# A mixture-of-experts decoder trunk on one core: the first expert's rows by one-hot products on the normed rows in SBUF

## Chip, cores, metric

The kernel runs on one core of one Trainium2 chip. The metric is the time of one execution on the device in microseconds (us); lower is better.

## What is computed

The input is 512 tokens (four tiles of 128, T = 4) of 1024 float32 features. There are two layers: gated linear attention, then forgetting attention, each followed by a grouped mixture of 16 experts of which each token takes two. The channel mixer is what the change touches:

```python
def grouped_moe(x, router_w, router_bias, w_gate, w_up, w_down):
    scores = softmax(x @ router_w); sel = scores + router_bias
    ...  # best group of 4 experts by the sum of its top 2, then the top 2 in it
    gates = sum(one_hot(expert_idx, N_EXPERTS) * w[..., None], axis=1)
    h = silu(einsum('td,edf->tef', x, w_gate)) * einsum('td,edf->tef', x, w_up)
    return einsum('tef,efd->td', h * gates[..., None], w_down)
```

Before it stands `h = layer_norm(ALPHA * h + mix, ...)`, after it `h = layer_norm(ALPHA * h + ffn, ...)`. The kernel computes each expert only for the tokens that picked it.

## The kernel before

One program per engine, written out by hand; semaphores join them, and each engine runs its instructions in order. SyncE loads weights, GpSimd gathers and scatters rows, TensorE multiplies, ScalarE and VectorE split every float32 operand into a high part (a cast to fp32r, by ScalarE) and a low part (the rest, by VectorE). A product of two such operands is three fp32r products (`products`, lines 717 to 719).

**Weights.** An expert has three matrices (gate, up, down), each in two halves of 1 MB. SyncE's `experts` (line 506) issues the 96 halves of a layer in the order gate 0, up 0, gate 1, up 1, down 0, gate 2 and so on, into eight raw halves of a ring. Halves 0 to 7 wait for the ring to be free, half 4 also for the stores of the normed rows (`last_rows_stored`), half 6 also for the first gather (line 499). From half 8 on, each waits for the half eight before it to be used (`half_used`). ScalarE casts a half (`high_half`, line 1346), VectorE takes its low part (`low_half`, line 1613), then TensorE may use it.

**Entry to the experts**, once in each layer. The last tile's norm ends; its rows stand in SBUF as `Hp` (tokens on partitions), and GpSimd stores all rows in DRAM as `h_rows` (line 593). TensorE computes the router's logits (line 822) and fills its time with products that nobody reads (`idle_products`, line 797). VectorE's `router` selects two experts per token with some twenty small instructions; ScalarE's Exp (line 1329) stands among them. `picked_b` goes to TensorE, which sums ranks (line 833: how many tokens up to this one picked the expert) and totals (line 836). VectorE masks the ranks (line 1774) and compares them with 1 to 128 (`one_hots4`, line 2233): for an expert a table of token by slot, 128x512. Four small products of this table with `info` (row numbers and gates) give the tokens of the slots (line 878, columns 0 and 1, `ids_done`) and, later, their gates (columns 2 and 3). VectorE turns them into row numbers `tokv` (line 1721) and `tokg` (line 1833).

**Rows of an expert.** GpSimd gathers 128 rows from `h_rows` by `tokv` into `xg` (line 607), which lies over the first two tiles of `Hp` and is cleared by two memsets first (line 586), since slots without a token are not written. TensorE transposes them in eight steps (`turn_rows`, line 885) into PSUM banks 0 and 1, ScalarE casts them (line 1356), VectorE takes the low part (line 1827), and `xgT` is ready: the gate product may start. At the entry, the gathers of experts 0 and 1 go out at once, that of expert 2 when expert 0 is transposed.

**The expert loop.** TensorE's order for expert e is: gate e, transposes of the rows of e+1, up e, down e-1, transposes of the hidden rows of e (`turn_hidden`, line 894, which waits for VectorE's gated product, line 1856), table of e+3 (line 870). ScalarE also writes the scaled residual to `sum_rows` in DRAM (line 1365), on which the experts' results are scattered with addition.

Of the kernel before, what the change touches and what calls it, by code (L numbers as in the profile page):

```python
# [5 lines left out]
F32 = mybir.dt.float32  # L6
# [4 lines left out]
ALU = mybir.AluOpType  # L11
ACT = mybir.ActivationFunctionType
AX = mybir.AxisListType
# [30 lines left out]
def yoco_trunk(nc, x, gla_w_in, gla_w_gk, gla_b_gk, gla_norm_g, gla_w_out, kv_w, forget_bias, fox_w_qg,  # L44
# [88 lines left out]
    with ctx:  # L133
# [116 lines left out]
        ranks = at(17792, T, E)  # L250
# [5 lines left out]
        IDS_BANKS = (7, 2, 3)  # L256
# [6 lines left out]
        rt = [at(14656 + 64 * n, T, E) for n in range(12)]  # L263
        rs = [at(14656 + 64 * 12 + 16 * n, T, GROUPS) for n in range(8)]
        rv = [at(14656 + 64 * 14 + 4 * n, T) for n in range(8)]
        total = at(14656 + 64 * 14 + 32, E)[0:1, :]
# [36 lines left out]
        pads_clear = sem("pads_clear")  # L303
        moves = sem("moves")
        hot, ids_done, tbl_done, tbl_ev = sem("hot"), sem("ids_done"), sem("tbl_done"), sem("tbl_ev")
# [146 lines left out]
        def _(sp):  # L452
# [35 lines left out]
            def experts(L):  # L488
                for n in range(HALVES):
# [4 lines left out]
                    elif n < RAW_HALVES:  # L494
# [3 lines left out]
                        if n == 6:  # L498
                            sp.wait_ge(gathered[0], 16 * (8 * L + 1))
# [27 lines left out]
        def _(pool):  # L527
# [54 lines left out]
            def clear_pads(L):  # L582
                pool.wait_ge(first_rows_stored, 32 * (L + 1))
                pool.wait_ge(h_scaled, T * L + 2)
                for n in range(2):
                    pool.memset(xg[:, n, :], 0.0).then_inc(pads_clear, 1)

            def layer_norm_rows(N):

                for t in range(T):  # L590
# [4 lines left out]
                    if t == 2:  # L595
                        clear_pads(N // 2)
# [105 lines left out]
        def _(pe):  # L702
# [91 lines left out]

            def idle_products(n, bank):
# [31 lines left out]
            def router(L):  # L827
                idle_products(20, 4)
                pe.wait_ge(rt_picked, L + 1)
                for t in range(T):  # L830
                    for s in range(t + 1):
                        before = upto_b if s == t else ones_b
                        pe.matmul(ps[:, 6, t * E:(t + 1) * E], before[:, :], picked_b[:, s, :],
                                  start=s == 0, stop=s == t)
# [4 lines left out]
                idle_products(5, 4)  # L839
# [22 lines left out]
            def experts(L):  # L862
# [13 lines left out]
                def entry_table(e, what, dst):  # L876
                    for s in range(T):
                        mm = pe.matmul(dst, onehot_of(e)[:, s * P:(s + 1) * P], info[:, s, e, what],
# [1382 lines left out]
```

## Time and profile before

| | us |
|---|---|
| median of the timed runs | 1234.52 |
| timed runs, lowest and highest | 1226.4, 1235.66 |
| the profiled execution's own time | 1230.52 |
| its span (first to last instruction) | 1228.8 |
| TensorE busy in it | 1193.8 (97%) |
| VectorE busy | 893.2 (73%) |
| ScalarE busy | 703.7 (57%) |
| GpSimd busy | 183.9 (15%) |

The span is what the trace shows; the time also holds what lies around it. Starts in the trace count from the span's start. Layer 0 enters its experts at about 250 to 285, layer 1 at about 890 to 925. PE is TensorE's matmuls, PEld its weight loads, DVE is VectorE, ACT ScalarE, POOL GpSimd, SPq SyncE's queue; "q" behind an engine is its sequencer. "x8" behind an entry is the number of records merged in it; a bracket at the end tells how long the engine was idle before it and what ended that.

### The profile page before, as it was taken

The numbers are of one execution on the slowest core, as the hardware profiler recorded it, in microseconds if no ns is written. First come the engines' busy times: TensorE is split into PE (matmuls) and PEld (weight loads), VectorE is DVE, ScalarE is ACT, GpSimd is POOL, SyncE is SP. The second block draws the span as 40 slices with busy tenths as digits, with TensorE's granted clock in tenths as the row PEclk, the third lists the DMA queues.
The fourth block names the chain that finished last, engine by engine and source line by source line (L and its number), as shares of the span: only waits on it lengthen the run. The fifth ranks groups of instructions, "written<-read, shape, count | busy, mean of one in ns | idle before, by whom it ended". The sixth has DMA issues, their size and how long they took to land.

```text
span 1228.8 us, 14990 instructions
## 1 busy us (share of the span) xinstructions
PE 1193.8 (97%) x5802; PEld 945.0 (77%) x5803; DVE 893.2 (73%) x1159; ACT 703.7 (57%) x866; POOL 183.9 (15%) x158
## 2 busy tenths in 40 slices
PE   7999999999999999999999999999999999999995
PEld 5787588877888888876887766768878888888873
DVE  5275555678999998989433555675679999998886
ACT  4432523357687786774333554573267778777672
POOL 1000100211132221210000000000212222122111
PEclk9999999999999999999899999999999999999998
DMA  8223021179999999987111420322289999999973
GB/s 286 71 85 122 1 103 70 52 257 411 358 368 378 368 370 377 358 340 281 69 70 52 154 86 18 103 84 88 78 314 381 373 362 376 379 367 371 370 276 137
DMA packets 66346, 281.52 MB, mean 229 GB/s; under 512 B 12854, under 2 KB 13110, under 8 KB 41698
## 3 DMA queue, kind: packets, MB, share of 16 engines
q1 hardware_dynamic: 49248, 247.55, 53.2%
q0 software_dynamic: 12288, 28.42, 8.1%
q10 hardware_dynamic: 4738, 4.57, 1.1%
q8 instruction: 47, 0.77, 0.3%
q14 instruction: 25, 0.20, 0.0%
HBM read 270.99 MB, written 25.20 MB: 241 GB/s over the span
## 4 chain that ended last, share of the span: by engine, by line
PE 83%; DMA 7%; DVE 6%; issue 2%; ACT 1%; POOL 0%; DVEq 0%; SPq 0%; ACTq 0%; POOLq 0%
PE ps L717 22%; PE ps L719 22%; PE ps L718 22%; DMA ring<-in_moe_w_up_dram 4%; PE ps L885 2%; PE ps L1168 2%; PE ps L1178 2%; DVE ring_r L1613 2%; PE ps L1191 2%; DMA ring<-in_moe_w_down_dram 1%; PE ps L894 1%; DMA ring<-in_kv_w_dram 1%; PE ps L822 1%; PE ps L1099 1%; PE ps L1087 1%
## 5 line engine op out<-in xcount | busy, mean ns | idle before, releaser
L1613 DVE TENSOR_TENSOR ring_r<-ring,ring_r 128x2048 fp32r<-128x2048 f32 x128 | 291.7, 2284 | 7.8 <-ACT ring_r L1346 7.8
L1346 ACT CAST ring_r<-ring 128x2048 fp32r<-128x2048 f32 x128 | 242.6, 1927 | 15.7 <-DMA ring<-in_moe_w_gate_dram 9.8
L718 PE MATMUL ps<-ring_r,xgT_r 128*128 128x512 f32 x528 | 205.9, 390 | 0.0
L1346 ACT CAST high_r<-ring 128x2048 fp32r<-128x2048 f32 x64 | 122.2, 1913 | 113.4 <-DMA ring<-in_moe_w_up_dram 113.4
L1613 DVE TENSOR_TENSOR ring_r<-ring,high_r 128x2048 fp32r<-128x2048 f32 x64 | 146.1, 2289 | 36.3 <-ACT high_r L1346 35.9
L613 POOL DMA_INDIRECT sum_rows<-arena,tokv x28 | 57.7, 2062 | 389.6 <-ACT arena L1399 389.6
L718 PEld LDWEIGHTS ps<-ring_r,xgT_r 128*128 128x128 f32 x528 | 99.3, 188 | 18.8
L717 PE MATMUL ps<-ring_r,xgT_r 128*128 128x512 f32 x272 | 109.1, 401 | 0.2 <-DVE ring_r L1613 0.2
L719 PE MATMUL ps<-ring_r,xgT_r 128*128 128x512 f32 x272 | 106.1, 390 | 0.0
L717 PE MATMUL ps<-high_r,xgT_r 128*128 128x512 f32 x256 | 102.9, 402 | 1.2 <-DVE xgT_r L1827 1.1
L717 PE MATMUL ps<-featT,ring_r 128*128 128x512 f32 x256 | 103.8, 405 | 0.0
L717 PE MATMUL ps<-ring_r,featT 128*128 128x512 f32 x256 | 102.4, 400 | 0.0
L1607 DVE TENSOR_TENSOR ring_r<-ring,ring_r 128x1024 fp32r<-128x1024 f32 x72 | 84.4, 1221 | 23.3 <-ACT ring_r L1259 23.3
L718 PE MATMUL ps<-ring_r,featT 128*128 128x512 f32 x256 | 100.3, 392 | 0.0
L719 PE MATMUL ps<-ring_r 128*128 128x512 f32 x256 | 100.3, 392 | 0.0
L719 PE MATMUL ps<-high_r,xgT_r 128*128 128x512 f32 x256 | 100.1, 391 | 0.0
L719 PE MATMUL ps<-featT,ring_r 128*128 128x512 f32 x256 | 100.1, 391 | 0.0
L718 PE MATMUL ps<-ring_r 128*128 128x512 f32 x256 | 99.8, 390 | 0.0
L717 PE MATMUL ps<-ring_r,hidT_r 128*128 128x512 f32 x240 | 93.8, 391 | 1.0 <-DVE ring_r L1613 1.0
L719 PE MATMUL ps<-ring_r,hidT_r 128*128 128x512 f32 x240 | 93.5, 390 | 0.0
L718 PE MATMUL ps<-ring_r,hidT_r 128*128 128x512 f32 x240 | 93.4, 389 | 0.0
L607 POOL DMA_INDIRECT arena<-h_rows,tokv x32 | 70.6, 2205 | 69.9 <-DVE tokg L1821 37.9
(288 smaller groups left out, 2118.8 us busy)
## 6 DMA issues: line engine op xcount, KB each, us to landing
ring<-in_moe_w_gate_dram SPq DMA_DIRECT2D x64, 1024.0 KB, 12.2
ring<-in_moe_w_up_dram SPq DMA_DIRECT2D x64, 1024.0 KB, 13.0
ring<-in_moe_w_down_dram SPq DMA_DIRECT2D x64, 1024.0 KB, 12.4
ring<-in_gla_w_in_dram SPq DMA_DIRECT2D x6, 2048.0 KB, 9.8
ring<-in_kv_w_dram SPq DMA_DIRECT2D x4, 2048.0 KB, 12.8
ring<-in_fox_w_qg_dram SPq DMA_DIRECT2D x4, 2048.0 KB, 8.1
ring<-in_gla_w_out_dram SPq DMA_DIRECT2D x2, 2048.0 KB, 7.8
h_rows<-arena POOLq DMA_DIRECT2D x8, 512.0 KB, 2.9
```

Source lines behind the costliest of these rows:

```text
L607: pool.indirect_dma_start(out=dst, out_offset=None, in_=h_rows, in_offset=bass.IndirectOffsetOnAxis(ap=rows, axis=0), bounds_check=last_ro ...
L613: pool.indirect_dma_start(out=sum_rows, out_offset=bass.IndirectOffsetOnAxis(ap=rows, axis=0), in_=src, in_offset=None, bounds_check=last_ ...
L717: pe.matmul(o, left[0], right[0], start=k == 0, stop=False)
L718: pe.matmul(o, left[0], right[1], start=False, stop=False)
L719: return pe.matmul(o, left[1], right[0], start=False, stop=k == n_k - 1)
L885: mm = pe.transpose(ps[:, kk, j * P:(j + 1) * P], src[:, (4 * kk + j) * P:(4 * kk + j + 1) * P], ident[:, :])
L1168: pe.matmul(ps[:, SCORE + a, 0:(i + 1) * P], kq[rows, p % 3, 1, i * P:(i + 1) * P], kq[rows, p % 3, 0, 0:(i + 1) * P], start=True, stop=Tr ...
L1178: mm = pe.transpose(ps[:, TURNED + a, n * P:(n + 1) * P], prob[:, s % 3, a, n * P:(n + 1) * P], ident[:, :])
L1191: mm = pe.matmul(ps[a * DH:(a + 1) * DH, VALUE, n * P:S], v_b[:, n, c:c + DH], prob_t[:, a, n, n * P:S], start=n == 0, stop=n == T - 1, sk ...
L1346: act.copy(high, w).then_inc(half_high, 1)
L1607: dve.tensor_tensor(low, w, high.bitcast(F32), ALU.subtract).then_inc(w_low, 1)
L1613: dve.tensor_tensor(low, w, high.bitcast(F32), ALU.subtract).then_inc(half_low, 1)
```

## The change

The rows of each layer's first expert (expert 0) are no longer gathered and transposed. TensorE multiplies `Hp`, still in SBUF, with expert 0's one-hot table: for each of the eight feature blocks, the sum over four token tiles of a product with 128x128 stationary and 128 moving float32 columns. The result is expert 0's rows already transposed, in banks 0 and 1. Around it:

- The table of expert 1 is the first one, behind the products; those of expert 2 and 0 stand behind expert 0's gate. Row numbers and gates are taken from one product of four columns. The first gather is that of expert 1, the next that of expert 2. Each has its wait: the one for expert 1 for all direct products (`xt_done`), since `xg` lies over `Hp`.
- The memsets of `xg` go. SyncE's half 6 waits for the gather of expert 1 (`gathered[1]`).
- ScalarE casts half 2 ahead of Exp and half 3 behind the row numbers of `info`; both casts stood behind the router.
- VectorE takes the low parts of halves 2 and 3 behind expert 0's rows, with the small table instructions around them.
- Five fillers after the ranks become four, and the fillers between and behind the tables go. The router's scratch moves from the arena to the place of `turned`.

```diff
             def router(L):
                 idle_products(20, 4)
                 pe.wait_ge(rt_picked, L + 1)
...
                 mm.then_inc(rt_ranks, 1)
-                idle_products(5, 4)
+                idle_products(4, 4)
...
+            def direct_rows(kk, tiles):
+
+                for j in range(4):
+                    c = slice(j * P, (j + 1) * P)
+                    for t in tiles:
+                        mm = pe.matmul(ps[:, kk, c], Hp[:, t, (4 * kk + j) * P:(4 * kk + j + 1) * P],
+                                       onehot_of(0)[:, t * P:(t + 1) * P].bitcast(F32),
+                                       start=t == 0, stop=t == T - 1, skip_group_check=True)
+                return mm
...
+                pe.wait_ge(hot, E * L + 1)
+                for kk in range(2):
+                    direct_rows(kk, range(EARLY, T)).then_inc(xt_done, 1)
                 pe.wait_ge(rt_info, 2 * (L + 1))
-                for e in range(3):
-                    pe.wait_ge(hot, E * L + e + 1)
-                    entry_table(e, slice(0, 2), ps[:, IDS_BANKS[e], 0:2]).then_inc(ids_done, 1)
-                    idle_products(2, 4)
                 pe.wait_ge(rt_ready, L + 1)
-                for e in range(3):
-                    entry_table(e, slice(2, 4), ps[:, 6, 2 * e:2 * e + 2]).then_inc(tbl_done, 1)
-                idle_products(5, 4)
-                pe.wait_ge(gathered[0], 16 * (8 * L + 1))
-                turn_rows(xg[:, 0, :], xt_done)
-                idle_products(4, 4)
+                entry_table(ENTRY[0])
                 for e in range(E + 1):
                     if e < E:
                         pe.wait_ge(xt_ev, 2 * (E * L + e + 1))
                         wide(ps[:, 2, :], xgT[:, e % 2, :, :], "gate", e)
+                    if e == 0:
+                        entry_table(ENTRY[1])
+                        pe.wait_ge(rt_total, L + 1)
+                        entry_table(ENTRY[2])
                     if e + 1 < E:
-                        pe.wait_ge(gathered[(e + 1) % 2], 16 * (8 * L + (e + 1) // 2 + 1))
+                        pe.wait_ge(gathered[(e + 1) % 2], 16 * ((7 + (e + 1) % 2) * L + e // 2 + 1))
                         turn_rows(xg[:, (e + 1) % 2, :], xt_done)
```

With `EARLY = 0` and `ENTRY = (1, 2, 0)`. On SyncE, GpSimd, ScalarE and VectorE:

```diff
                         if n == 6:
-                            sp.wait_ge(gathered[0], 16 * (8 * L + 1))
+                            sp.wait_ge(gathered[1], 16 * (8 * L + 1))
...
-                pool.wait_ge(pads_clear, 2 * (L + 1))
+                pool.wait_ge(first_rows_stored, 32 * (L + 1))
+                pool.wait_ge(h_scaled, T * L + 2)
                 pool.wait_ge(last_rows_stored, 32 * (L + 1))
-                for e in range(3):
-                    pool.wait_ge(tbl_ev, 2 * E * L + e + 1)
-                    if e == 2:
-                        pool.wait_ge(xt_done, 2 * (E * L + 1))
+                pool.wait_ge(xt_done, 2 * (E * L + 1))
+                for n, e in enumerate(ENTRY[:2]):
+                    pool.wait_ge(tbl_ev, 2 * (E * L + n) + 1)
                     gather(xg[:, e % 2, :], tokv[:, e, 0:1], gathered[e % 2])
...
             def router(L):
+                high_half(L, 2)
...
+                high_half(L, 3)
                 scale_residual(L, T - 1)
...
-                high_half(L, 2)
-                high_half(L, 3)
                 take_rows(0)
...
+                take_rows(0)
+                take_entry(0)
                 low_half(L, 2)
-                take_rows(0)
                 low_half(L, 3)
+                take_entry(1)
+                take_entry(2)
                 low_half(L, 4)
                 low_half(L, 5)
```

TensorE's order in layer 0 between the totals and the first gate product, before. `picked_b` is the selection, `high_r` stands in the fillers, `featT` is the memory in which the one-hot tables and `info` lie, `arena` that of `xg`.

```order
L797 MATMUL ps<-high_r 128x512 x5
L878 MATMUL ps<-featT 128x2 [waits hot,rt_info]
L878 MATMUL ps<-featT 128x2 x3
L797 MATMUL ps<-high_r 128x512 x2
L878 MATMUL ps<-featT 128x2 [waits hot]
L878 MATMUL ps<-featT 128x2 x3
L797 MATMUL ps<-high_r 128x512 x2
L878 MATMUL ps<-featT 128x2 [waits hot]
L878 MATMUL ps<-featT 128x2 x3
L797 MATMUL ps<-high_r 128x512 x2
L878 MATMUL ps<-featT 128x2 [waits rt_ready]
L878 MATMUL ps<-featT 128x2 x11
```

Ahead of them stand the totals of line 836, behind them five fillers, the eight transposes (they wait for `gathered0`), four fillers and the gate. After, from the totals on:

```order
L846 MATMUL ps<-picked_b,ones_b 128x16 x4
L810 MATMUL ps<-high_r 128x512 x4
L803 MATMUL ps<-featT,arena 128x128 [waits hot]
L803 MATMUL ps<-featT,arena 128x128 x31
L889 MATMUL ps<-featT 128x4 [waits hot,rt_ready,rt_info]
L889 MATMUL ps<-featT 128x4 x3
L712 MATMUL ps<-high_r,xgT_r 128x512 [waits half_low,xt_ev]
```

The tables, fillers and transposes have given way to 32 products (one with a wait, 31 behind it, `arena` being `Hp`) and one table; the last row is the first gate product, line 717 of before. Behind the 24 products of gate 0, TensorE's order after the change has:

```order
L889 MATMUL ps<-featT 128x4 [waits hot]
L889 MATMUL ps<-featT 128x4 x3
L889 MATMUL ps<-featT 128x4 [waits hot,rt_total]
L889 MATMUL ps<-featT 128x4 x3
L896 MATMUL ps<-ident,arena 128x128 [waits gathered1]
L896 MATMUL ps<-ident,arena 128x128 x7
L712 MATMUL ps<-ring_r,xgT_r 128x512 [waits half_low]
```

Before, only the transposes of expert 1 stood there (they wait for `gathered1`); now two tables stand ahead of them.

ScalarE's order in layer 0 from the last logits' copy on, before; `ring` and `ring_r` are a raw half and its high part.

```order
L1329 ACT_TABLE_LOAD
L1329 ACTIVATE arena<-arena 128x64 [waits rt_in]
L1331 CAST featT<-row_id 128x64 x2
L1301 ACTIVATE resid<-arena 128x8x128 [waits ln_ready]
L1334 ACT_TABLE_LOAD
L1334 ACTIVATE ln_r<-half 128x1
L1336 COPY arena<-ps 1x16 [waits rt_ranks]
L1346 CAST ring_r<-ring 128x2048 [waits w_free,half_loaded2]
L1346 CAST ring_r<-ring 128x2048 [waits w_free,half_loaded3]
```

After, from the same place:

```order
L1357 CAST ring_r<-ring 128x2048 [waits w_free,half_loaded2]
L1339 ACT_TABLE_LOAD
L1339 ACTIVATE turned<-turned 128x64 [waits rt_in]
L1341 CAST featT<-row_id 128x64 x2
L1357 CAST ring_r<-ring 128x2048 [waits w_free,half_loaded3]
L1310 ACTIVATE resid<-arena 128x8x128 [waits ln_ready]
L1345 ACT_TABLE_LOAD
L1345 ACTIVATE ln_r<-half 128x1
L1347 COPY arena<-ps 1x16 [waits rt_ranks]
```

The cast of half 2 has moved ahead of the table load and Exp, that of half 3 ahead of the residual's scaling.

## Rows read from the trace of the kernel before

**Rows 1.** The page, part 4: the chain that ended last, by engine.
```profile
PE 83%; DMA 7%; DVE 6%; issue 2%; ACT 1%; POOL 0%; DVEq 0%; SPq 0%; ACTq 0%; POOLq 0%
```

**Rows 2.** TensorE's timeline at both layers' entry: start us, us, line, op, tiles.
```profile
267.18 1.09 PE L885 MATMUL ps<-ident,arena 128*128 128x128 f32 x8 [0.80 <-DMA arena<-h_rows,tokv]
...
269.83 0.50 PE L717 MATMUL ps<-high_r,xgT_r 128*128 128x512 f32 x1 [0.63 <-DVE xgT_r L1827]
...
275.41 1.04 PE L885 MATMUL ps<-ident,arena 128*128 128x128 f32 x8
...
289.61 1.03 PE L885 MATMUL ps<-ident,arena 128*128 128x128 f32 x8
...
909.50 0.50 PE L717 MATMUL ps<-high_r,xgT_r 128*128 128x512 f32 x1 [0.48 <-DVE xgT_r L1827]
```

**Rows 3.** VectorE's timeline of both layers' entry, columns as above.
```profile
259.82 0.23 DVE L1774 TENSOR_TENSOR arena<-ps,arena 128x64 f32<-128x64 f32 x1 [0.29 <-PE ps L836]
260.08 1.29 DVE L2233 TENSOR_TENSOR featT<-slot,arena 128x512 fp32r<-128x512 f32 x2
261.54 0.16 DVE L1721 TENSOR_SCALAR tokv<-ps 128x2 uint32<-128x2 f32 x1 [0.16 <-PE ps L878]
...
282.00 1.12 DVE L1856 SCALAR_TENSOR_TENSOR arena<-arena,tokg,ps 128x512 f32<-128x512 f32 x1 [3.82 <-issue]
...
283.05 4.47 DVE L1613 TENSOR_TENSOR ring_r<-ring,high_r 128x2048 fp32r<-128x2048 f32 x2
...
899.05 0.22 DVE L1774 TENSOR_TENSOR arena<-ps,arena 128x64 f32<-128x64 f32 x1 [0.29 <-PE ps L836]
```

**Rows 4.** The chain in order of time, 259 to 285: start us, us, what.
```profile
262.68 4.46 DMA arena<-h_rows,tokv
...
283.84 0.34 PE ps L870 x4
```

**Rows 5.** Windows of layer 1: busy us of PE, PEld, DVE, ACT, POOL; clock, DMA, GB/s.
```profile
904.45:907.90 3.45, 3.45 (x14) 2.73 (x13) 2.43 (x4) 0.52 (x1) 0.00 (x0) 0.51 0.64 176
...
915.10:923.80 8.70, 7.43 (x42) 6.11 (x40) 4.83 (x6) 5.43 (x6) 0.00 (x0) 1.00 1.02 423
```

**Rows 6.** Attention scores, line 1065: its instructions, and the timeline of eight.
```profile
L1065 PE MATMUL ps<-arena x32: 275/275/377, 107.1 to 136.4; 128*128 128x128 f32 x32
...
117.45 1.16 PE L1065 MATMUL ps<-arena 128*128 128x128 f32 x8
```

**Rows 7.** SyncE's line 506, halves 2 and 3, layer 0 then layer 1.
```profile
L506 SPq DMA_DIRECT2D ring<-in_moe_w_up_dram x2: 328/380/433, 248.2 to 248.5; - x2
...
DMA to landing us min/median/max: 5.1/6.1/7.1
...
L506 SPq DMA_DIRECT2D ring<-in_moe_w_up_dram x2: 327/380/432, 887.4 to 887.8; - x2
...
DMA to landing us min/median/max: 5.0/6.0/7.0
```

**Rows 8.** ScalarE's timeline of both layers' entry.
```profile
252.94 1.28 ACT L1329 ACT_TABLE_LOAD   x1
255.51 0.26 ACT L1329 ACTIVATE arena<-arena 128x64 f32<-128x64 f32 x1 [1.29 <-DVE arena L1738]
...
258.17 1.28 ACT L1334 ACT_TABLE_LOAD   x1
259.47 0.20 ACT L1334 ACTIVATE ln_r<-half 128x1 f32<-128x1 f32 x1
...
280.62 1.90 ACT L1346 CAST high_r<-ring 128x2048 fp32r<-128x2048 f32 x1 [1.19 <-DMA ring<-in_moe_w_up_dram]
...
894.73 0.26 ACT L1329 ACTIVATE arena<-arena 128x64 f32<-128x64 f32 x1 [2.60 <-DVE arena L1738]
```

**Rows 9.** GpSimd's line 607, the gather of expert 1, window 264.0 to 264.5.
```profile
DMA to landing us min/median/max: 5.0/5.0/5.0
```

**Rows 10.** The same line, the gather of expert 3, window 289 to 290.
```profile
DMA to landing us min/median/max: 9.7/9.7/9.7
```

More of the change, by code:

```diff
@@ L249, in yoco_trunk @@
         dummy = at(18000, P)
-        ranks = at(17792, T, E)
+        ranks = at(18464, T, E)
         spare = hT_hi[:, :, :].rearrange("p k s -> p (k s)")
@@ L793, in tail, with rank @@
                 entry_end(L)
+            def rank(L, t):
+                bank = 6
+                for s in range(t + 1):
+                    before = upto_b if s == t else ones_b
+                    mm = pe.matmul(ps[:, bank, t * E:(t + 1) * E], before[:, :], picked_b[:, s, :],
+                                   start=s == 0, stop=s == t)
+                return mm
[6 more added lines that the diff above has]
+                                       start=t == 0, stop=t == T - 1, skip_group_check=True)
+                return mm
             def idle_products(n, bank):
@@ L829, in router @@
                 pe.wait_ge(rt_picked, L + 1)
[L830 to L834, printed above, removed]
+                for t in range(EARLY, T):
+                    rank(L, t)
                 for s in range(T):
@@ L1327, in router @@
             def router(L):
-                act.wait_ge(rt_in, L + 1)
-                act.activation(rt[1], rt[0], ACT.Exp).then_inc(rt_exp, 1)
+                high_half(L, 2)
+                act.wait_ge(rt_in, 1 * (L + 1))
+                act.activation(rt[1][:, EARLY:T, :], rt[0][:, EARLY:T, :], ACT.Exp).then_inc(rt_exp, 1)
                 for m in range(2):
@@ new lines, in some @@
+                def some(v):
+                    return v[:, t0:t1, :]
+                peak, whole, best, chosen = (v[:, t0:t1] for v in (rv[0], rv[1], rv[3], rv[4]))
+                logits = some(rt[11])
+                dve.wait_ge(rt_logits, turn)
+                dve.wait_ge(ln_rstd, 2 * L * T + t1)
+                do(dve.tensor_tensor(logits, ps[:, 6, t0 * E:t1 * E].rearrange("p (t e) -> p t e", t=T_),
+                                     over_e(ln_r[:, t0:t1, 1]), ALU.mult))
+                do(dve.tensor_tensor(logits, logits, each_t(shift_logits[:, L, :], E), ALU.add))
@@ new lines, in select @@
+                do(dve.tensor_reduce(peak, logits, AX.X, ALU.max))
+                dve.tensor_tensor(some(rt[0]), logits, over_e(peak), ALU.subtract).then_inc(rt_in, 1)
+                dve.wait_ge(rt_exp, turn)
+                weights, sel = some(rt[1]), some(rt[3])
+                do(dve.tensor_reduce(whole, weights, AX.X, ALU.add))
+                do(dve.tensor_tensor(some(rt[2]), over_e(whole), each_t(rbias[:, :], E), ALU.mult))
+                do(dve.tensor_tensor(sel, weights, some(rt[2]), ALU.add))
@@ new lines, in take_ranks, with router, over_e @@
+            def take_ranks(L, t0, t1, turn):
+                dve.wait_ge(rt_ranks, turn)
+                bank = 6
+                do(dve.tensor_tensor(ranks[:, t0:t1, :],
+                                     ps[:, bank, t0 * E:t1 * E].rearrange("p (t e) -> p t e", t=t1 - t0),
+                                     rt[8][:, t0:t1, :], ALU.mult))
+            def router(L):
+                def over_e(v):
+                    return v.unsqueeze(2).to_broadcast([P, T, E])
+                turn = 1 * (L + 1)
+                select(L, EARLY, T, turn)
+                do(dve.tensor_tensor(rt[9], rt[1], rt[8], ALU.mult))
@@ L1779, in router @@
-                one_hots4(dve, onehot_of(2), hot, ranks, slot1, 2)
-                take_ids(L, 1)
                 do(dve.reciprocal(rv[6], rv[5]))
@@ L1785, in router @@
                                   ).then_inc(rt_ready, 1)
+                one_hots4(dve, onehot_of(2), hot, ranks, slot1, 2)
             def count_parts(L):
```

104 lines of the change are left out of this document (42 added, 62 removed).

## Prediction

> **What bounds the kernel now.** I read the page's chain first: TensorE holds most of it, DMA and VectorE a few per cent each [rows 1]. So only what moves TensorE's start, or makes it wait, can move the time. Next the TensorE timeline around the two places where a layer enters its experts: the eight transposes of expert 0 at 267.18, its first gate product at 269.83 in layer 0 and at 909.50 in layer 1, the transposes of expert 1 at 275.41 [rows 2]. Then VectorE: the masked ranks at 259.82 and 899.05, a one-hot table behind them [rows 3]. Between ranks and first gate product lie 10.01 us in layer 0 and 10.45 us in layer 1; that stretch is what the change rebuilds. Its largest piece in the chain is the gather of expert 0, 4.46 us from issue to landing [rows 4]. The clock windows say why layer 1 is longer: TensorE was granted 0.51 of its clock (its lower level, 1.2 GHz) from 904.45 to 907.90 [rows 5], behind tables that are two columns wide.
>
> **Products for the gather and transposes.** The 32 products have a float32 stationary operand of 128x128 and 128 moving float32 columns. The trace of before has this form in the attention scores of line 1065: 16 products in the program are 32 records in the trace, so two records for one product, and eight records take 1.16 us with the last alone 0.275 us [rows 6]. That is (1.16 - 0.275) / 7 = 0.126 us a record. 64 records end 63 x 0.126 + 0.275 = 8.21 us after the first starts. The first starts when the one-hot table of expert 0 is there: 0.26 us from the rank product to the table, 0.65 us for it (half of 1.29 us for two), 0.16 us more to TensorE's first use, with rounding 1.10 us [rows 3]. Behind the last product stand ScalarE's second cast and VectorE's second low part, as before: from the transposes' end (267.18 + 1.09) to 269.83 is 1.56 us [rows 2]; I take 1.5. New stretch: 1.10 + 8.21 + 1.5 = 10.81 us. Against before: +0.80 us in layer 0, +0.36 us in layer 1. The first half's cast hides beside the second half's products.
>
> The lower bound of a product, from a nearer limit: the 128x128 transposes are one record each and eight take 1.04 us [rows 2], (1.04 - 0.275) / 7 = 0.109 us, which would save 64 x 0.017 = 1.1 us a layer. The upper bound is the half clock: the same at 1.2 GHz for the 3.45 us of one such window loses about 1.7 us. I take the row of the same form.
>
> The Trainium skill ("FP8 and Floating Point Precision", TensorE Precision Notes) says that a true float32 product is four passes through the array. By that, 128 columns at 2.4 GHz are 0.213 us a product and the 32 would take 6.8 us instead of 8.2; this trace has 2 x 0.126 = 0.252 us for a product of the form, and I keep that.
>
> **The cast moved ahead of Exp.** ScalarE now casts weight half 2 before it waits for the router's logits, and the table load for Exp stands behind that cast. In layer 0 the half is issued at 248.2 and lands 5.1 us later, at 253.3 [rows 7], 0.4 us after ScalarE is free (252.94, where the table load starts today) [rows 8]. A cast is 1.9 us, as the one at 280.62 [rows 8]; so cast to 255.22, load 1.28 us to 256.50, Exp at 256.55 instead of 255.51: +1.04 us, and everything down to the ranks waits for it. In layer 1 no load stands there, the half lands at 887.4 + 5.0 = 892.4, the cast ends at 894.3 and Exp started at 894.73 [rows 7, 8]: nothing, with 0.4 us to spare. If the halves landed as late as the pair's second (7.1 us), layer 0 would lose 3 us; if the load were overlapped, nothing. The cast of half 3 and the residual's scaling then end some 3 us later than now, hidden under the 8 us of products.
>
> The Trainium skill ("ScalarE: Activation LUTs", What ACT_TABLE_LOAD costs) adds a drain of about 1380 ns to each load of 1283 ns. By that Exp would be 1.4 us later still and the sum 1.4 us larger. The trace disagrees: the load at 258.17 takes 1.28 us and the activation runs at 259.47, 0.02 us behind it [rows 8].
>
> **Tables moved behind the first gate.** Expert 1's table stands behind the products, in the wait for casts: hidden. Those of experts 2 and 0 stand between gate and transposes of expert 1, on TensorE's path: four products are 0.34 us in the chain [rows 4], so +0.68 us a layer. VectorE has two waits more, with halves 4 and 5, a one-hot table and expert 1's rows queued behind. From the first gate product G: halves 2 and 3 take 4.47 us (a pair), the wait ends at about G + 6.4, then 4.47 + 0.65 + 1.29 us bring it to G + 12.85 [rows 3]. TensorE is ready for the gated product at G + 5.58 + 0.68 + 6.59 = G + 12.85 (275.41 - 269.83, and 282.00 - 275.41) [rows 2, 3]. VectorE had 3.8 us of slack there and now has none, but costs nothing yet. TensorE's wait at 282 stays.
>
> **Expert 1's gather.** It was issued early and landed unseen. Now its row numbers come behind expert 0's low parts, at G; the gather starts 1.1 us later, as expert 0's did (261.54 to 262.68) [rows 3, 4], and must land by G + 6.26. In a quiet stretch one took 5.0 us [rows 9], under the full stream of weights 9.7 us [rows 10]. Now only the four writes of the residual run beside it, no weights. From 5.0 (wait 0) to 9.7 us (wait 4.5) I take 5.5 us, near the quiet row: +0.35 us a layer.
>
> **SyncE's wait.** Halves 6 and 7 now wait for that gather: at G + 6.6, that is 278.3 in layer 0, where today they go out as expert 0's gather lands, at 262.68 + 4.46 = 267.1 [rows 4]. Alone a pair lands in 5.1 and 7.1 us [rows 7]: so by about 285.8, cast by 287.7 and with its low part by 290.0. They are needed behind the transposes of expert 2, which end at 290.6 now [rows 2] and some 3 us later then. Hidden, by about 3 us. The two memsets on GpSimd cost nothing today: what ended its wait for the first gather was the row numbers, not they.
>
> **Sum.** Layer 0: 0.80 + 1.04 + 0.68 + 0.35 = 2.9 us. Layer 1: 0.36 + 0.68 + 0.35 = 1.4 us. Together +4.3 us; nothing later takes it back, since TensorE does not wait for long in the expert loop. The profiled execution took 1230.52 us, of which 1228.8 are its span; it lies 4.0 below the median of the three timed runs (1234.52). The four runs have a mean of 1231.8, which I take as the level: 1236.1 us.
>
> **Rivals.** (a) The gather meets the residual's writes and takes 9.7 us: TensorE waits 4.5 us instead of 0.35 before the transposes of expert 1, in both layers, and halves 6 and 7 come later still. +4.3 + 8.3 = +12.6 us, 1244.4 us. For it: the same DMA rings, 2 MB of writes issued just ahead. Against: the 5.0 us row and no weights in flight. It decides from 5.2 us of landing time, 1 us a layer for each further us. (b) The dropped filler products let the clock fall once a layer: 2 x 1.7, +7.7 us, 1239.5 us. Against: TensorE idled in the stretch up to 923.80 too, at clock 1.00 [rows 5]; the stream of products is denser than the two-column tables. (c) The products run faster than the row of line 1065: 0.109 us a record, and Exp is not delayed. +4.3 - 2.2 - 1.0 = +1.1 us, 1232.9 us. By the skill's four passes it is 2 x 1.4 us less instead of 2.2. (d) A real gain: products at half the price, 4.1 us, with Exp on time: 4.3 - 8.2 - 1.0 = -4.9 us, 1226.9 us. Only if two records ran as one; rows 6 speak against it.
>
> **How the numbers follow.** The forecast 0.60, (a) 0.12, (b) 0.10, (c) 0.14, (d) 0.04. About 1% (12.3 us) is what a measurement of this kernel can tell from no change. Only (a) reaches it, at its edge, so slower 0.08; faster 0.03; within 1% 0.89. The range goes from 1227 (case (d), and (c) with a low draw among runs that spread by 9 us) to 1246 (case (a)).
>
> **What would show it.** 64 records of the new products at 0.126 us; the table load behind a cast, Exp 1.0 us behind its input in layer 0 and on time in layer 1; first gate product 10.8 us after the ranks; two tables of 0.34 us ahead of expert 1's transposes and a wait below 1 us for the gather; SyncE's halves 6 and 7 some 10 us later with no wait of TensorE for them. It is wrong if TensorE waits more than 1.5 us for the gather, if the granted clock falls in the new stretch, or if the rest of the expert loop shows new waits on low halves.

## The result, and the profile after

The changed kernel takes 1240.43 us (median of 9 runs, 1237.68 to 1242.73). The kernel before has a median of 1232.18 us over 9 runs, the three of the table above and six made beside the changed kernel. The ratio is 1.0067, with a 95% interval of 1.0051 to 1.0083: 8.3 us slower (6.3 to 10.2), inside 1%. The forecast was +4.3 us and 1236.1; the time lies in the range (1227 to 1246) and within 1%, as forecast, but the loss is about twice the forecast.

The profiled execution took 1240.57 us with a span of 1238.9. The page's chain, which answers to [rows 1]:

```profile
PE 77%; DMA 10%; DVE 8%; ACT 2%; issue 2%; POOL 0%; DVEq 0%; SPq 0%; POOLq 0%; ACTq 0%
```

DMA and VectorE have grown in it. TensorE's timeline of both entries, the counterpart of [rows 2]:

```profile
252.22 1.90 PE L835 MATMUL ps<-rw,turned 128*128 128x16 f32 x16
...
259.91 0.18 PE L794 MATMUL ps<-picked_b,upto_b 128*128 128x16 bf16 x1 [1.12 <-DVE picked_b L1783]
...
261.54 7.41 PE L803 MATMUL ps<-featT,arena 128*128 128x128 f32 x64
268.70 0.59 PE L889 MATMUL ps<-featT 128*128 128x4 f32 x4
270.35 0.50 PE L712 MATMUL ps<-high_r,xgT_r 128*128 128x512 f32 x1 [1.06 <-DVE xgT_r L1856]
...
275.92 0.95 PE L889 MATMUL ps<-featT 128*128 128x4 f32 x8
278.12 1.09 PE L896 MATMUL ps<-ident,arena 128*128 128x128 f32 x8 [1.26 <-DMA arena<-h_rows,tokv]
285.99 0.66 PE L905 MATMUL ps<-ident,arena 128*128 128x128 f32 x4 [1.29 <-DVE arena L1884]
...
899.12 1.90 PE L835 MATMUL ps<-rw,turned 128*128 128x16 f32 x16
...
907.45 7.41 PE L803 MATMUL ps<-featT,arena 128*128 128x128 f32 x64
...
916.26 0.49 PE L712 MATMUL ps<-high_r,xgT_r 128*128 128x512 f32 x1 [1.06 <-DVE xgT_r L1856]
...
923.91 1.09 PE L896 MATMUL ps<-ident,arena 128*128 128x128 f32 x8 [1.13 <-DMA arena<-h_rows,tokv]
931.76 0.65 PE L905 MATMUL ps<-ident,arena 128*128 128x128 f32 x4 [1.28 <-DVE arena L1884]
```

I call *entry* the time from the start of the last tile's router logits (line 835) to the start of the transposes of expert 0's hidden rows (line 905): 33.77 us in layer 0 and 32.64 us in layer 1. The same two marks of the kernel before:

```profile
252.56 1.89 PE L822 MATMUL ps<-rw,turned 128*128 128x16 f32 x16
...
283.18 0.66 PE L894 MATMUL ps<-ident,arena 128*128 128x128 f32 x4 [1.28 <-DVE arena L1856]
...
891.77 1.90 PE L822 MATMUL ps<-rw,turned 128*128 128x16 f32 x16
...
922.89 0.66 PE L894 MATMUL ps<-ident,arena 128*128 128x128 f32 x4 [1.26 <-DVE arena L1856]
```

That is 30.62 and 31.12 us, so the entries cost +3.15 and +1.52 us. VectorE's marks split them (the counterpart of [rows 3]):

```profile
260.53 0.23 DVE L1788 TENSOR_TENSOR arena<-ps,turned 128x64 f32<-128x64 f32 x1 [0.29 <-PE ps L846]
...
284.80 1.14 DVE L1884 SCALAR_TENSOR_TENSOR arena<-arena,tokg,ps 128x512 f32<-128x512 f32 x1 [1.47 <-issue]
...
906.45 0.22 DVE L1788 TENSOR_TENSOR arena<-ps,turned 128x64 f32<-128x64 f32 x1 [0.29 <-PE ps L846]
```

| stretch | layer 0 before, after | layer 1 before, after | forecast |
|---|---|---|---|
| last logits to masked ranks | 7.26, 8.31 (+1.05) | 7.28, 7.33 (+0.05) | +1.04, 0 |
| masked ranks to first gate product | 10.01, 9.82 (-0.19) | 10.45, 9.81 (-0.64) | +0.80, +0.36 |
| first gate product to hidden rows | 13.35, 15.64 (+2.29) | 13.39, 15.50 (+2.11) | +1.03, +1.03 |

ScalarE in layer 0 shows why the first is late (counterpart of [rows 8]):

```profile
252.99 1.91 ACT L1357 CAST ring_r<-ring 128x2048 fp32r<-128x2048 f32 x1 [0.40 <-DMA ring<-in_moe_w_up_dram]
254.92 1.28 ACT L1339 ACT_TABLE_LOAD   x1
256.21 0.26 ACT L1339 ACTIVATE turned<-turned 128x64 f32<-128x64 f32 x1
```

GpSimd's gather of expert 1, first in layer 0, then in layer 1, in place of [rows 9] (its issue, and the time to landing):

```profile
L602 POOL DMA_INDIRECT arena<-h_rows,tokv x1: 2259/2259/2259, 271.4 to 271.4; - x1
...
DMA to landing us min/median/max: 6.7/6.7/6.7
...
L602 POOL DMA_INDIRECT arena<-h_rows,tokv x1: 2277/2277/2277, 917.2 to 917.2; - x1
...
DMA to landing us min/median/max: 6.6/6.6/6.6
```

It starts 1.0 us behind the first gate product and lands at 278.1, where TensorE has waited 1.26 us for it. The DMA queues show why it takes 6.7 us. q10 carries ScalarE's four writes of the residual, q0 the gather. From 269 to 275.2 only q10 moves data, then all 144 packets of the gather follow, from 275.2 to 278.2 (queue and its kind: packets, MB, share of the 16 DMA engines' time; first the one window, then the other):

```profile
q10 hardware_dynamic: 560, 2.10, 85.4%
```

```profile
q0 software_dynamic: 144, 0.28, 35.4%
q10 hardware_dynamic: 16, 0.00, 0.3%
```

In layer 1 it is the same: no packet of q0 between 914.9 and 920.9, while q10 moves 2.03 MB. So the gather is issued behind the writes and its data moves behind them.

Two more things differ between the two profiles. The expert loops (hidden rows of expert 0 to those of expert 15) take 273.6 and 273.5 us where they took 272.4 and 271.8. And the clock fell for longer around the narrow products behind layer 0's norm (64 products of 32 columns, `narrow`). The fall begins inside their run and lasts into the wide products behind them. Windows (columns as in [rows 5]) of before, ahead of the fall and over the stretch at half clock, then of after, over its stretch at half clock:

```profile
599.00:607.50 8.50, 8.50 (x65) 7.96 (x64) 2.49 (x4) 0.59 (x1) 0.00 (x0) 1.00 0.44 156
607.50:614.30 6.80, 6.80 (x26) 6.12 (x26) 0.64 (x3) 2.36 (x4) 0.00 (x0) 0.50 0.31 116
```

```profile
608.80:622.50 13.70, 13.70 (x55) 12.64 (x55) 0.87 (x4) 3.93 (x6) 0.00 (x0) 0.50 0.36 137
```

At half clock half of such a stretch is lost: 3.4 and 6.85 us. So the spans' difference of 10.1 us is 4.7 of entries, 2.9 of loops and 3.4 of clock, less 0.9 at the start, the end and between. The experiments ask which of these belongs to the change.

### The profile page after: what moved, and what is told of

Same layout as the page of the kernel before. It is cut to its first block, busy times and chain, and to the rows that moved or that the text cites. A ratio compares the mean times of both kernels' runs of the same rounds, so it can differ in the third digit from the quotient of the medians.

```text
span 1238.9 us, 15098 instructions
## 1 busy us (share of the span) xinstructions
PE 1197.2 (97%) x5858; PEld 950.0 (77%) x5859; DVE 892.7 (72%) x1159; ACT 702.2 (57%) x866; POOL 186.8 (15%) x152
## 4 chain that ended last, share of the span: by engine, by line
PE 77%; DMA 10%; DVE 8%; ACT 2%; issue 2%; POOL 0%; DVEq 0%; SPq 0%; POOLq 0%; ACTq 0%
PE ps L712 20%; PE ps L714 20%; PE ps L713 20%; DMA ring<-in_moe_w_up_dram 6%; DVE ring_r L1624 3%; PE ps L1177 2%; PE ps L1187 2%; PE ps L896 2%; PE ps L1200 1%; DMA ring<-in_moe_w_down_dram 1%; PE ps L803 1%; DMA arena<-h_rows,tokv 1%; PE ps L905 1%; PE ps L761 1%; DMA ring<-in_kv_w_dram 1%
## 5 line engine op out<-in xcount | busy, mean ns | idle before, releaser
L602 POOL DMA_INDIRECT arena<-h_rows,tokv x30 | 77.3, 2576 | 72.1 <-DVE tokg L1845 64.6
```

What stands on the lines that cost most here:

```text
L602: pool.indirect_dma_start(out=dst, out_offset=None, in_=h_rows, in_offset=bass.IndirectOffsetOnAxis(ap=rows, axis=0), bounds_check=last_ro ...
```

## The experiments

Twelve runs were made, two of them of the kernels unchanged; all stand here. Those with several timed runs are given as a ratio to the kernel before on the same chip, with its 95% interval; 0.001 is 1.2 us.

**Do the later halves 6 and 7 cost the loops their 1 to 1.6 us?** One kernel sends them early in the changed kernel, the other late in the kernel before.

```diff
 # x1_half6_early: the changed kernel
-                            sp.wait_ge(gathered[1], 16 * (8 * L + 1))
+                            sp.wait_ge(hot, E * L + 1)
 # x4_before_half6_late: the kernel before
-                            sp.wait_ge(gathered[0], 16 * (8 * L + 1))
+                            sp.wait_ge(half_used, half_count(L, 1))
```

> The changed kernel, with SyncE's half 6 waiting for expert 0's one-hot table instead of expert 1's gather. Marks: from the hidden rows' transposes of expert 0 to those of expert 15 (the loop) it is 272.4 us (layer 0) and 271.8 us (layer 1) before the change, 273.6 and 273.4 after it. Theory S (the loads of halves 6 and 7 went out 11 us later, the stock of loaded weights is smaller, and the loop pays where it runs out, at experts 10 to 12): loops back to 272.4 and 271.8 or less, the gather of expert 1 still lands in 6 to 7 us because both halves have landed before it starts; about 2.8 us less than the change, 1237.6 us. Rival R (the loop's loss is chance of that execution, or contention of another kind): loops within 0.3 us of 273.6 and 273.4, time 1240.4. Rival G: the gather is slower beside more weights, over 8 us, and what the loop wins the entry loses.

> The kernel before, with half 6 of each layer waiting until half 1 is used (275.4 in layer 0) instead of expert 0's gather (267.1): nothing else changed. Theory S: the entries stay (hidden rows of expert 0 at 283.2 and 922.9 of the trace), the loops grow by 1.0 to 1.6 us each, time about 1232.2 + 2.5 = 1234.7. Rival R: loops stay at 272.4 and 271.8 within 0.3 us, time 1232.2.

x1: 1244.33 us, ratio 1.0111 (1.0090 to 1.0132). x4: 1232.53 us, 1.0006 (0.9995 to 1.0017), its loops 272.7 and 272.1 us. So late halves alone cost some 1 us or nothing, at most 2. x4 does not test all of the delay: its halves 6 and 7 go out 5.8 us behind the first gate product (271.05 to 276.87), in the changed kernel 7.8 us (270.35 to 278.14). Early halves cost the entry more than they could win: x1's loops are 271.3 and 270.6 us, 2.4 and 2.9 shorter than the changed kernel's, but its entries are 39.4 and 37.3 us, 5.6 and 4.7 longer (with 6.8 and 3.4 us at half clock in them, half of which is lost). TensorE's timeline and the gather of x1 in layer 0:

```profile
281.96 1.97 PE L896 MATMUL ps<-ident,arena 128*128 128x128 f32 x8 [4.04 <-DMA arena<-h_rows,tokv]
```

```profile
L602 POOL DMA_INDIRECT arena<-h_rows,tokv x1: 2263/2263/2263, 272.4 to 272.4; - x1
...
DMA to landing us min/median/max: 9.5/9.5/9.5
```

The gather now runs beside weights as well as the writes and takes 9.5 us; TensorE waits 4.04 us (4.53 in layer 1). This is the size that rival (a) feared, but with another cause: (a) blamed the writes alone. SyncE's new wait keeps it away. Rival G of the expectation came true.

**What the moved cast and the tables cost.** x2 casts half 2 behind the Exp, x3 makes all three tables ahead of the first gate, y1 does both.

```diff
 # x2_exp_first (ScalarE)
-                high_half(L, 2)
                 act.wait_ge(rt_in, 1 * (L + 1))
 ...
+                high_half(L, 2)
                 high_half(L, 3)
 # x3_tables_first (TensorE)
                 entry_table(ENTRY[0])
+                entry_table(ENTRY[1])
+                pe.wait_ge(rt_total, L + 1)
+                entry_table(ENTRY[2])
 ...
-                    if e == 0:
-                        entry_table(ENTRY[1])
-                        pe.wait_ge(rt_total, L + 1)
-                        entry_table(ENTRY[2])
```

> The changed kernel, with the cast of half 2 put back behind Exp and the row numbers, just ahead of that of half 3. My step: the cast pushes the table load of Exp and with it layer 0 by 1.0 us. Then Exp runs at its input again (0.05 us behind VectorE's last logits), the first gate product comes 1.0 us earlier in layer 0 and the same in layer 1 or 0.3 us earlier. Rival: the load moves with the Exp anyway and ends 1.28 us behind the logits: gain below 0.3 us.

> The changed kernel, with all three tables of the entry behind the direct products, ahead of expert 0's gate. TensorE idled 1.06 us there, so two tables (0.7 us) fit in: the gate starts at the same time and the transposes of expert 1 could start 0.7 us earlier. If the wait for the gather decides (it landed 1.26 us after TensorE was free), the start of these transposes does not move and TensorE only waits longer there, 1.9 us; if the tables decide, 0.7 us less a layer. VectorE's path to the hidden product gets 0.8 us of slack more.

> The changed kernel with both of the looks before in one: the cast of half 2 behind the Exp, and the tables of experts 2 and 0 ahead of expert 0's gate. Theory (the gather of expert 1 decides when expert 0's up products begin): the 1.0 us of the Exp in layer 0 is won, the 0.95 us of the tables in each layer comes back as a longer wait of TensorE for the gather (2.0 us a layer), so 1.0 to 1.5 us under the changed kernel: 1239.0 (1238 to 1240). Rival (the tables decide): 2.9 us under it, 1237.5, with the waits for the gather at 1.3 us. If the two single looks' shorter expert loops (272.2 and 272.3 us with the tables moved) are real and not a profile's noise, 2 us more come off: 1237.

x2 and x3 were run once each, both 1239.64 us. In x2 Exp is on time and layer 0's entry is 32.80 us (252.61 to 285.41), 0.97 less than the changed kernel's: the cast's price, as forecast. In x3 the tables are off the path, and the wait for the gather takes their place (2.02 us, and 1.94 in layer 1, 0.8 more in each than in the changed kernel). Layer 1's entry stays what it was, 32.66 us:

```profile
270.69 1.48 PE L889 MATMUL ps<-featT 128*128 128x4 f32 x12
...
280.11 1.09 PE L896 MATMUL ps<-ident,arena 128*128 128x128 f32 x8 [2.02 <-DMA arena<-h_rows,tokv]
```

So the gather's start decides when expert 1's rows come, not the tables. y1: 1236.75 us, ratio 1.0049 (1.0029 to 1.0069), with waits of 2.07 us in both layers. The waits are as the theory has them. The time is 2.3 us under its 1239.0 as it stands, but the kernel before took 1231.21 us on this chip, and as a ratio the theory is 1.0055, inside the interval. The profile's loops were 270.6 and 271.2 us, as in the clause on shorter loops; one profile, of the fastest of the six runs, does not decide that.

**Freeing the gather.** y2 is y1 with expert 1's rows gathered into the idle result buffer, so that they need not wait for the products that still read the normed rows, and with its table between the two halves of the products.

```diff
 # TensorE
-                for kk in range(2):
-                    direct_rows(kk, range(EARLY, T)).then_inc(xt_done, 1)
+                direct_rows(0, range(EARLY, T)).then_inc(xt_done, 1)
                 pe.wait_ge(rt_info, 2 * (L + 1))
                 pe.wait_ge(rt_ready, L + 1)
                 entry_table(ENTRY[0])
+                direct_rows(1, range(EARLY, T)).then_inc(xt_done, 1)
 ...
-                        turn_rows(xg[:, (e + 1) % 2, :], xt_done)
+                        turn_rows(xg[:, (e + 1) % 2, :] if e else yb[:, 1, :], xt_done)
 # GpSimd; yb[:, 1, :] is cleared once ahead of this, in layer 0
-                pool.wait_ge(xt_done, 2 * (E * L + 1))
 ...
                     pool.wait_ge(tbl_ev, 2 * (E * L + n) + 1)
+                    if n == 1:
+                        pool.wait_ge(xt_done, 2 * (E * L + 1))
-                    gather(xg[:, e % 2, :], tokv[:, e, 0:1], gathered[e % 2])
+                    gather(xg[:, 0, :] if n else yb[:, 1, :], tokv[:, e, 0:1], gathered[e % 2])
 # VectorE
-                take_rows(0)
                 take_entry(0)
+                take_rows(0)
```

> As y1, and expert 1's gather freed from the direct products: its rows go to a buffer that nothing else uses then, its table stands between the two halves of the direct products, so the gather is issued about 5 us earlier (near 266.5 in layer 0 where the changed kernel has 271.4), and so are halves 6 and 7. Theory (the entry's loss is the gather's late start): no wait of TensorE ahead of expert 1's transposes, entry about 3.5 us shorter in layer 0 and 2.5 in layer 1 than the changed kernel's, so 1234.5 if the loops stay as long as the changed kernel's, 1232 if the loops' extra 1.2 and 1.6 us came from transfers that all began late behind that gather. Rival (the gather 5 us earlier runs beside the last residual writes or weights and takes 9 us and more): it still lands before 277 and the entry is the same. Rival (the entry does not matter, the rest is noise): 1240, as the changed kernel.

1233.17 us, ratio 1.0008 (0.9993 to 1.0022). It was timed on the chip of y1. GpSimd's timeline and the gather's landing, then TensorE's timeline of layer 0:

```profile
265.97 1.13 POOL L603 DMA_INDIRECT arena<-h_rows,tokv  x1 [10.05 <-DVE tokg L1849]
...
DMA to landing us min/median/max: 4.4/4.4/4.4
```

```profile
252.30 1.90 PE L840 MATMUL ps<-rw,turned 128*128 128x16 f32 x16
...
275.44 1.04 PE L901 MATMUL ps<-ident,arena 128*128 128x128 f32 x8
...
283.20 0.66 PE L910 MATMUL ps<-ident,arena 128*128 128x128 f32 x4 [1.27 <-DVE arena L1888]
```

No wait stands before expert 1's transposes, and both entries are 30.9 us, 2.9 and 1.8 us shorter than the changed kernel's (expected were 3.5 and 2.5). Six to seven of the eight microseconds are gone (2.0 us are left by the medians, 1.0 by the ratio), though the same 32 products are still on the path. The step from y1 to y2 is the gather's start and the place of its table alone. From the last logits to expert 1's transposes y1 takes 24.90 and 24.93 us and y2 23.14 and 23.11, 3.6 us less in both layers together; the medians are 1236.75 and 1233.17, 3.6 us apart (5.0 by the ratios, give or take 3). So the late gather's price is shown in the trace and in the time. The loops took 272.9 us each here, no shorter than with a late gather, which speaks against the theory's second half.

**The clock in the narrow products.** The 64 products are spread out, 16 behind each tile's wide ones, in the kernel before (z1), in the changed one (z3) and in y2 (z2).

```diff
                 unit(U_FOX + t, frees=1 if t == T - 1 else 0, ks=range(K // 2, K))
-            for t in range(T):
                 mm = narrow(t, gkf)
             mm.then_inc(fl_done, 1)
```

> The kernel before, with the 64 narrow products behind layer 0's norm no longer in one run: 16 stand behind each tile's wide products. Theory (the half clock falls on the long run of narrow products, 6.8 us of it in the kernel before, half of which is lost): no stretch at half clock there, 3.4 us off the profile's span, 1229 against 1232. Rival (the clock falls there for another reason, such as the wait for the norm ahead of it, or the narrow products count the same wherever they stand): a stretch of 3.4 to 6.8 us at half clock stays between 600 and 625 us and the time is within 1 us of the kernel before.

> The changed kernel with the same edit (16 narrow products behind each tile's wide products). Its profile had 13.65 us at half clock there, the kernel before 6.83. Theory (that is 3.4 us of the difference between the two kernels): about 6.8 us off the changed kernel, 1233.6, and the difference to the kernel before with the same edit is 4.5 to 7.5 us, made of the entries (4.7) and the loops (0 to 2.8). Rival (the longer half clock is an accident of the profiled executions, both kernels lose 6.8 to 13.7 us of clock in timed runs alike): the edit wins the same in both kernels and their difference stays 8.2 us.

> The version with the early gather (1233.2, 2.0 us over the kernel before) and 16 narrow products behind each tile's wide products (4.7 us off the kernel before, 5.2 off the changed one). If the two add up: 1228.4, faster than both kernels, but 2 us behind the kernel before with the same edit (1226.5). Rival (the narrow edit takes away a stall in one version that the other does not have): equal to it or faster, 1225 to 1227.

| kernel | us | ratio to before |
|---|---|---|
| z1, before + edit | 1226.52 | 0.9959 (0.9940 to 0.9978) |
| z3, changed + edit | 1235.21 | 1.0033 (1.0022 to 1.0045) |
| z2, y2 + edit | 1227.96 | 0.9972 (0.9958 to 0.9987) |

Windows of z1, then of z3 over the stretch where the clock fell before:

```profile
600.00:640.00 40.00, 40.00 (x201) 33.26 (x201) 15.83 (x20) 14.71 (x20) 0.64 (x1) 1.00 0.30 101
```

```profile
600.00:640.00 40.00, 40.00 (x209) 33.46 (x208) 13.90 (x18) 15.65 (x22) 0.35 (x1) 1.00 0.17 56
```

The fall is gone in both, and both gain the same within the noise, 5.1 and 4.2 us by the ratios, 4.7 and 5.2 by the medians. z3 and z1 stay 8.7 us apart (9 by the ratios). So the rival holds: the 3.4 us of clock between the two profiles are not the change's. (z3's profiled execution, 1238.11 us, was the slowest of its 12; in it the clock fell in layer 1's entry instead, for 10.2 us from 891.5 and 3.5 from 922.2.) z1 beats both kernels, and z2 does too, 1.4 us behind z1: the early gather and the spread products add up, as expected (1228.4).

**Both kernels unchanged, a second profile of each.**

> The kernel before, unchanged, for a second profile. If the half clock in the narrow products behind layer 0 and the length of the expert loops belong to the kernel: again 6.8 us at half clock near 607, loops of 272.4 and 271.8 us. If they belong to the execution: another length of half clock there (0 to 13.7 us) or loops that differ by 0.5 us and more.

> The changed kernel, unchanged, for a second profile. If the longer half clock (13.7 us) and the longer loops (273.6 and 273.4 us) belong to the change: the same again. If they belong to the execution: one of the loops within 0.5 us of the kernel before's, or less half clock. The entries (33.8 and 32.7 us from the last logits to expert 0's hidden rows) stay the same within 0.3 us either way.

w1 took 1234.99 us, w2 1241.28. Windows of w1, then of w2:

```profile
250.70:254.10 3.40, 3.39 (x15) 3.20 (x15) 2.12 (x1) 1.97 (x3) 0.87 (x2) 0.51 1.00 422
609.10:619.30 10.20, 10.20 (x40) 9.31 (x40) 0.64 (x3) 3.33 (x6) 0.00 (x0) 0.50 0.34 130
```

```profile
251.30:261.50 10.20, 10.20 (x38) 8.94 (x37) 5.99 (x19) 7.87 (x9) 1.19 (x3) 0.50 0.76 288
282.10:285.50 3.40, 3.40 (x13) 3.00 (x12) 3.40 (x3) 1.67 (x3) 1.81 (x1) 0.50 0.79 243
613.10:623.30 10.20, 10.20 (x41) 9.33 (x41) 0.65 (x3) 3.11 (x5) 0.00 (x0) 0.50 0.35 134
```

Both kernels now have the same 10.2 us at half clock in the narrow products. The loops are 274.2 and 272.7 us in w1, 271.2 and 272.8 in w2: this time the kernel before has the longer ones. So neither the clock there nor the loops belong to the change; both vary from one execution to the next by as much as I had found between the kernels. In all fourteen profiles the loops are 270.6 to 274.2 us. The first seven steps from one expert to the next take 18.1 or 18.2 us in each; the difference lies in the later ones. Layer 1's entry is the same again in w2 (32.67 us), as expected. Layer 0's is not: 37.9 us, since the clock fell inside it, a case that my expectation left out.

**What a microsecond on the entry costs.** v1 makes the direct products twice.

```diff
                 for kk in range(2):
+                    direct_rows(kk, range(EARLY, T))
                     direct_rows(kk, range(EARLY, T)).then_inc(xt_done, 1)
```

> The changed kernel with the 32 direct products of each layer made twice, the second time over the first, so each layer's entry grows by 64 more records of TensorE, 7.4 us by the 0.1158 us a record measured in its profile, all on the path; the gather, the tables and halves 6 and 7 start that much later. Theory (a microsecond on the entry costs a microsecond at the end, whatever the expert loops do): 14.8 us over the changed kernel's 1240.4, so 1255.2 (1253.5 to 1257). Rival (an entry that is late costs more than itself, because the transfers that start behind it are late too; this would explain why the difference of 8.2 us is more than the 5.4 us that the entries show): over 1258, with loops longer than 273.5 us in both layers. Rival (the weights catch up meanwhile and the loops' stalls at experts 10 to 12 shrink): 1250 to 1253, with loops of 270.5 to 271.5 us.

1254.49 us, ratio 1.0177 (1.0154 to 1.0200): 14.1 us over the changed kernel by the medians, 13.6 by the ratios. The row of its products:

```profile
262.20 14.56 PE L803 MATMUL ps<-featT,arena 128*128 128x128 f32 x128
```

14.56 - 7.41 = 7.15 us more a layer, 14.3 in both. The loops took 271.4 and 273.8 us, 272.6 on the mean, where the three profiles of the changed kernel with and without the narrow edit have 272.5. So, within the some 3 us to which these ratios hold, the entry's microseconds come through one for one, neither taken back nor multiplied by the loops.

## Why the prediction was right, and where it was not

**The bound: right.** What moves TensorE's start of the expert work, or makes it wait there, moves the time; v1 shows it at a price of one for one, y1 and y2 for the wait.

**The products: right in kind, 10% too dear.** They are two records each, as [rows 6] had it, but a record costs (7.41 - 0.275) / 63 = 0.113 us (v1: (14.56 - 0.275) / 127 = 0.112), where the prediction took 0.126 from the eight records of line 1065. The lower bound from the transposes, 0.109, was the nearer row. The moving columns do not seem to set this pace: the records of the narrow products, 32 columns each, start 0.112 us apart too (602.15 to 607.29 us in the kernel before, 46 steps). So 7.41 us stand where 8.21 were forecast, and the stretch from ranks to gate became 9.8 us, shorter than before, instead of 10.81: rival (c)'s first half came true. A product is 0.227 us. The Trainium skill ("FP8 and Floating Point Precision", TensorE Precision Notes) says four passes, by which 0.213 us is an estimate. The trace lies between that and my row, closer to the skill's.

**Exp behind the cast: right.** +1.05 us in layer 0 (forecast 1.04), next to nothing in layer 1. x2 takes the microsecond back. The load ends and the activation starts 0.01 us later (254.92 + 1.28 to 256.21). The Trainium skill ("ScalarE: Activation LUTs", What ACT_TABLE_LOAD costs) gives a drain of about 1380 ns beside each load, for every switch to another set of tables. It shows in no row here.

**The tables: 0.95 us for eight products, where 0.68 was forecast, and not what decided.** The 0.34 us of [rows 4] are only the part of a table's products that the chain counted, from 283.84. The timeline of the same four starts them at 283.59, and the next product starts at 284.04, 0.45 us later:

```profile
283.59 0.59 PE L870 MATMUL ps<-featT 128*128 128x4 f32 x4
```

x3 moved the tables off the path and the wait for the gather grew by 0.8 us.

**The gather: the term that was mis-sized.** I took 5.5 us of latency, near the quiet row, and a wait of 0.35 us. It took 6.7 and 6.6 us with its packets behind the residual's 2 MB of writes, and TensorE waited 1.26 and 1.13 us, above the 1 us named as a sign of being right and below the 1.5 us of being wrong. That is between the forecast and rival (a), which needed 9.7 us; x1 shows nearly that figure (9.5) as soon as weights run beside it. (a) named the right cause, the writes issued just ahead, though not "the same DMA rings": gather and writes go through two queues, q0 and q10. The entries came out at +4.7 us against +4.3 forecast by luck: the stretch with the products was forecast too long by 1.0 us in each layer, wait and tables too short by 1.3 and 1.1 us, and the errors cancel.

**SyncE's halves, VectorE's lost slack: hidden, as forecast.** x4 bounds most of the first (1.0006, its interval ends at +2.1 us). VectorE still waits 1.47 us ahead of the gated product in the changed kernel, where the forecast left it none, against the 3.82 us of [rows 3]; TensorE's wait behind it is 1.29 where it was 1.28.

**"Nothing later takes it back": right (v1), but the sum does not reach 8.3 us.** The entries account for 4.7 us, or 5.3 if the kernel before is taken with its clock whole in layer 1: in z1 the entry there is 30.5 us, since the half clock of [rows 5] is missing. The loops average 272.6 us over the profiles of the kernel before, w1 and z1, and 272.5 over those of the changed one, w2 and z3, single ones 271.1 to 274.2; so they add nothing that can be seen. What remains is about 3 us, or 1 to 5.5 by the ratio's interval.

The clock, rival (b), explains little of it. In the profiles it seems to: in the eight with a late gather (the changed kernel, w2, x1, x2, x3, y1, z3, v1) it stood at half for 0 to 11.6 us between the entries' marks, 5.9 on the mean; in the four of the kernel before, w1, x4 and z1 for 0 to 4.3 us, 2.1 on the mean; in y2 and z2 never. It can fall in the new products too: in x3's layer 0 they took 8.87 us instead of 7.41. Half of the 3.8 us between the means would be 1.9 us. But each timed run has a mean granted clock on record, and there are many more of these than profiles. One minus that mean, times the span, is the time lost to the clock. The mean is 0.9911 over the 9 runs of the changed kernel, which is 11.0 us lost, and 0.9901 to 0.9909 over the runs of the kernel before beside the experiments, 11.1 to 12.2 us lost. So these runs give the clock no share in the 8.3 us. With the narrow products apart it may account for a part: 0.9945 in z3 and 0.9956 in z1, 6.8 and 5.4 us lost, 1.4 of 8.7 us.

So some 3 us of the loss stay without a cause. They may lie in the loops: six single values of each kernel leave their sum over both layers uncertain by some 3 us. A late gather is not all of it either: y2, whose entries together are as long as those of the kernel before (61.8 and 61.7 us), is still 1 to 2 us slower.

## What to carry to other kernels

A latency that moves from ahead of a stage to beside it is free only if its start is early enough: here the products were as fast as the gather and transposes they replaced, and the largest part of the loss that has been traced (3.6 of some 8 us) came from the next gather. It had to wait for a buffer that those products read, its row numbers were made behind the products (they came last: GpSimd's wait ended with `tokg`, line 1845), and by then 2 MB of writes were queued ahead of it. Give the next transfer a buffer of its own and its row numbers first, ahead of the writes, and the wait is gone; which of the three weighs most was not tried apart. And profile both kernels at least twice before explaining a difference of a few microseconds in a long loop or in the clock: two of the three pieces that the first pair of profiles showed belonged to the executions.

## What the runs showed that I had not expected

- 64 products of 32 columns in one run let the granted clock fall to 0.50 (1.2 GHz) for 6.8 to 13.7 us in each of the eleven profiles in which they stand together. Idle time did not bring the fall: in the kernel before TensorE was busy for 8.50 of the 8.50 us ahead of it. With 16 behind each tile's wide products it stays at 1.00 (2.4 GHz) there in all three, worth some 5 us.
- The same kernel can lose the clock in one execution and keep it in the next in the same stretch: layer 0's entry was 33.8 us in one profile of the changed kernel and 37.9 in the other.
- The gather of 128 rows takes 4.4 us when it is issued ahead of the writes (y2), 6.7 when it is issued behind 2 MB of them, its packets moving only when theirs are through, and 9.5 to 9.7 with weights in flight (x1, [rows 10]).
